# Where the split weights of a two-model fp32 kernel lie in SBUF, modulo 512 bytes

## The reference, cut to what matters

```
def swiglu(x, w_in, w_out):
    a, b = jnp.split(x @ w_in, 2, axis=-1)
    return (jax.nn.silu(a) * b) @ w_out
...
h = h + 0.5 * swiglu(rmsnorm(h, norm_ffn1), w_ffn1_in, w_ffn1_out)
fq, fk, fv, ff, rq, rk, rv, rg, ga, gb = jnp.split(u @ w_in, IN_SPLITS, axis=-1)
...
x = layer_norm(ALPHA * x + g2 * swiglu_2(modulate(x, sh2, sc2), w_ffn_in[l], w_ffn_out[l])) * ln2_g[l] + ln2_b[l]
```

## The kernel before, in words

| tile | start modulo 512 before | after |
|---|---|---|
| token tiles (X1 to X5, H1 to H4, O, MX, TH, TL) | 320 | 320 |
| Wbase, high and low | 128 | 128 |
| Wtop, high and low | 128 | 64 |
| Wlatent, high and low | 128 | 192 |
| Wmixed, high and low, and PAm | 128 | 192 |
| Wvalues, high and low | 64 | 64 |
| CS, RT | 128, 256 | 64, 192 |

## Time and profile before

### The profile page before, as it was taken

One profiled execution on the slowest core, in us unless ns is written; L12 is line 12 of the kernel. 1 busy time (PEld: TensorE's weight loads), 2 busy tenths in 40 slices (PEclk: granted clock), 3 DMA queues, 4 the chain that ended last, 5 costly groups with the idle time before them and its releaser, 6 DMA issues. The chain is left out here.

```text
span 3286.8 us, 60350 instructions
## 1 busy us (share of the span) xinstructions
PE 3163.5 (96%) x24442; PEld 2940.6 (89%) x24458; DVE 1802.9 (55%) x3099; ACT 1391.2 (42%) x2533; POOL 481.6 (15%) x471
## 2 busy tenths in 40 slices
PE   7999999999999999999999999999999999989998
PEld 7999988797778899998889888999998889979997
DVE  4666643536744456666435774222326645776765
ACT  4222232336633342224447755212125547664544
POOL 1010110036500010110103301101010103111110
PEclk9999999999999999999999999999999999999999
DMA  4445422122223244543210341221214321425653
GB/s 155 173 163 178 154 71 78 58 75 61 58 68 96 85 141 173 180 172 129 72 42 21 110 130 53 70 65 59 71 59 122 101 62 40 147 77 149 166 147 102
DMA packets 107074, 339.68 MB, mean 103 GB/s; under 512 B 12144, under 2 KB 16496, under 8 KB 106672
## 3 DMA queue, kind: packets, MB, share of 16 engines
q1 hardware_dynamic: 97616, 311.65, 29.3%
q0 software_dynamic: 8752, 23.65, 3.2%
q10 hardware_dynamic: 432, 0.52, 0.0%
HBM read 324.38 MB, written 2.10 MB: 99 GB/s over the span
## 5 line engine op out<-in xcount | busy, mean ns | idle before, releaser
L2716 DVE TENSOR_TENSOR r_Wbasel<-r_Wf,r_Wbaseh 128x1024 fp32r<-128x1024 f32 (+3 forms) x286 | 359.7, 1259 | 506.5 <-ACT r_Wbaseh L2012 506.2
L2012 ACT ACTIVATE r_Wbaseh<-r_Wf 128x1024 fp32r<-128x1024 f32 (+3 forms) x286 | 291.3, 1022 | 425.8 <-PE PS L1331 318.1
L1329 PE MATMUL PS<-r_X1h,r_Wbaseh 128*128 128x264 f32 (+1 forms) x848 | 286.6, 338 | 12.5 <-DVE r_X1l L3064 5.1
L2716 DVE TENSOR_TENSOR r_Wtopl<-r_Wf,r_Wtoph 128x1024 fp32r<-128x1024 f32 (+3 forms) x147 | 174.5, 1189 | 203.7 <-ACT r_Wtoph L2012 203.5
L1329 PE MATMUL PS<-r_X2h,r_Wbaseh 128*128 128x256 f32 (+1 forms) x888 | 274.3, 309 | 6.2 <-POOL r_X2l L3675 2.6
L1330 PE MATMUL PS<-r_X1l,r_Wbaseh 128*128 128x264 f32 (+1 forms) x848 | 273.6, 323 | 0.0
L1331 PE MATMUL PS<-r_X1h,r_Wbasel 128*128 128x264 f32 (+1 forms) x848 | 273.5, 323 | 0.0
L1330 PE MATMUL PS<-r_X2l,r_Wbaseh 128*128 128x256 f32 (+1 forms) x888 | 266.7, 300 | 0.0
L1331 PE MATMUL PS<-r_X2h,r_Wbasel 128*128 128x256 f32 (+1 forms) x888 | 266.6, 300 | 0.0
L2012 ACT ACTIVATE r_Wtoph<-r_Wf 128x1024 fp32r<-128x1024 f32 (+3 forms) x147 | 146.0, 1001 | 140.1 <-PE PS L1331 57.3
L1329 PEld LDWEIGHTS PS<-r_X1h,r_Wbaseh 128*128 128x128 f32 x848 | 160.5, 189 | 33.7 <-issue 8.0
(11 more groups left out here) (535 smaller groups left out, 10665.1 us busy)
## 6 DMA issues: line engine op xcount, KB each, us to landing
r_Wf<-in_wmod SPq DMA_DIRECT2D x96, 512.0 KB, 3.6
r_Wf<-in_f_in SPq DMA_DIRECT2D x88, 512.0 KB, 4.4
r_Wf<-in_g_in SPq DMA_DIRECT2D x69, 512.0 KB, 3.6
r_Wf<-in_w_o SPq DMA_DIRECT2D x40, 512.0 KB, 4.5
r_Wf<-in_f_out SPq DMA_DIRECT2D x32, 448.0 KB, 4.2
r_Wf<-in_g_out SPq DMA_DIRECT2D x32, 448.0 KB, 3.4
r_SR<-in_g_in SPq DMA_DIRECT2D x38, 256.0 KB, 3.5
r_SR<-in_g_in POOLq DMA_DIRECT2D x38, 256.0 KB, 5.4
```

The costliest lines, as they stand in the source:

```text
L1329: self.e.matmul(o, wh, xh, start=first, stop=False)
L2012: e.activation(p.w(i, cols)[0], p.Wf[:, i % NW, 0:cols], ACT.Copy).then_inc(*p.hi.did(i))
L2716: e.tensor_tensor(l, p.Wf[:, i % NW, 0:cols], h.bitcast(F32), ALU.subtract).then_inc(*p.lo.did(i))
```

## The change

The start of the top slots goes down by 64 bytes, and with it that of CS and RT. The start of the mixed and the latent slots goes up by 64 bytes, and with it PAm, a small tile of partial sums behind the mixed slots. No instruction is added, removed or moved, no wait changes, and the order of the work stays. The whole diff:

```diff
-TOP = 187904
+TOP = 187840
...
-        p = self.weight_slots("mixed", 3, P2 + 320)
+        p = self.weight_slots("mixed", 3, P2 + 384)
...
-        self.weight_slots("latent", 2, p + 320)
+        self.weight_slots("latent", 2, p + 384)
```

## The result

The changed kernel takes 3335.81 us (median of 4 runs, 3329.72 to 3340.27) against 3290.96 us for the kernel before in the same comparison: ratio 1.0116, 95% interval 1.0084 to 1.0148. It is slower, by 1.2% by that ratio and by 1.4% by the medians, and lies 37 us above the forecast of 3299 us and above the forecast range, which ended at 3325 us.

A forecast was written before the change was run, and what follows sets the result against it. Matmuls, busy 96% of the span, were taken to bound the kernel; +7 us for top, latent and mixed slots, 0 for the rest, on 3288.65 us gave 3295.7 us, or 3299 us as a median 3.8 us higher; range 3280 to 3325 us.

The forecast's parts named there:

- Two paces, and a stall that chooses between them: 256-column matmuls: start every 113.4 or 117.6 ns; a stall draws the pace anew, which then stays for many items.
- the term of +7 us: Top, latent and mixed slots, 6162 matmuls of 256 columns: slow share goes from 24% to 50%, +7 us.
- the bound of +20 us: Top, latent and mixed slots: if the new offset held all 4680 fast matmuls at the slow pace, +20 us.
- a pace of over 118 ns at the new offset: Undisturbed stretch: a pace under 113 or over 118 ns at the new offset would show the forecast wrong.
- The row I leaned on: First block's first stages, 264 columns: 122 ns with a moving offset against 116.7 ns estimated, 5 ns lost.
- Base slots, taken as 0: Unmoved base slots, about 6160 matmuls: 0 taken, ends of +18 us if disturbed and -9 us if freed.
- rival 3: 256-column matmuls turn slow at offset 256: +20 us for top slots alone, +38 us with base items dragged along; chance 0.22.
- Latent and mixed slots: Weight slots the change moves to 192 modulo 512: 128 from the tokens, not 256 as its description says.
- 264 columns, VectorE, ScalarE, CS, RT, PAm: nothing: Other parts: 264 columns within -3 to +3 us, VectorE's 6 ns a tile hidden, small tiles nothing.
- Waits that absorb: Stalls on late weights or splits could take back what TensorE gains or loses, 4 ns in a matmul.
- The rule of the two ports: TensorE's SBUF reads: separate ports for moving operand and weights, so the offset can't matter and the sum would be 0.
- The prediction's -26 us: Top, latent and mixed slots: if offset 256 reached the skill page's 262 cycles, 6162 x 4.2 ns = -26 us.

The follow-up runs named there:

- E5: Bare matmul stream, not the kernel: finer offsets, twelve stalls, weights moved between items, 264 and 512 columns; at 192, 113.3 or 117.8 ns a matmul.
- E1: Bare stream of three-matmul steps, not the kernel: tokens 0 to 480 bytes above weights, behind three stalls; 113.3 ns at 192, 120.0 ns at 256.
- E3: Against the kernel before: token tiles up 64 bytes, all weight slots at 128 modulo 512, so every set lies 256 from the tokens; 3343.39 us, ratio 1.0165.
- E8: Against the kernel before: only the top slots moved, 64 bytes up, to offset 128 from the tokens; 3313.37 us, ratio 1.0056.

## Why the prediction was wrong

1. **Two paces, and a stall that chooses between them.** Right. E5 has both at 192, by the stall alone.
2. **Top slots, the term of +7 us.** This is the step that failed. It said that a new offset keeps the two paces of 192 and changes at most the share of each. But 256 has a pace of its own, 120.0 ns, and no other, in every run. The true term is 33 us. Even the bound of +20 us was too low, because I took 117.6 ns for the slowest pace there is. The prediction named a pace of over 118 ns at the new offset as a sign that it was wrong, but gave it no term in the sum; the sign came.
3. **The row I leaned on.** I called the 264-column matmuls the nearest row, estimated 116.7 ns for them at rest and put the other 5 ns down to their walking offset. E5 measured 120.0 ns for 264 columns at 192 at rest. So the row said nothing about offsets. A column count is no stand-in for another one. The trace of before had no steady stream of 256 columns at 256, and I should have made the upper bound wider for that.
4. **Base slots, taken as 0.** Wrong, measured +18 us. The upper end I gave was +18 us, and the mechanism was the one rival 3 named: the items between are dragged along. It had a chance of 0.22 and is what happened, with its first part 13 us too small. That the two 18 agree is partly luck: by the mean distances about 22% of the base matmuls were slow before, not 33%, and about 82% after, not all. And the range was cut at 3325 us though rival 3 reached 3330 us; even that end lies 6 us under the result.
5. **Latent and mixed slots.** They do lie 128 from the tokens, as worked out, and not 256. Both run at 118.6 ns; together 1.5 us.
6. **264 columns, VectorE, ScalarE, CS, RT, PAm: nothing.** Right: 0.6 us on 264 columns, VectorE busy within 0.5 us.
7. **Waits that absorb.** Named as what could spoil the sum; they took 6 to 8 us of 53.
8. **The rule of the two ports.** The Trainium skill, "TensorE: Matmul & The Clock Gate", section "Step-by-step: what each phase is for", has weight loads take nothing from the running matmul. E1 measured 113.3 and 120.0 ns for the same instructions, with no other engine at work between the stalls, by the offset alone; here the measurement decides, though no run shows which read waits for which. The Trainium skill, same page, section "Back-to-back issue gap", gives the 262 cycles for a single isolated matmul and says that in a stream of weight loads and matmuls both set the spacing. The prediction's -26 us used that figure for a stream. In the streams here no offset reached 262: the least for 256 columns was 272.

Why 192 modulo 256 is the good place, what the 16, 26.7 or 32 cycles beyond the 256 are spent on, and why the return from 256 is slow when the weights move and fast when the tokens do, stays open. So does what the exchange of the two operands changes (last section). The runs show that it is so and no more.

## What to carry to other kernels

When stationary and moving operands of a long stream of fp32r matmuls have a fixed address offset, that offset modulo 256 is worth trying as a tuning parameter. Here 192 against 256 made 6% of a matmul's pace, and 1.6% of the whole kernel when every set lay at 256 (E3). Measure a bare stream at each offset, behind several stalls, for each column count in use, before laying out tiles. Keep all slots that alternate inside a stage on one offset modulo 256, since here one set at 256 slowed another that had not moved. And where the trace has no row of the new state, don't take the worst state it does have for a bound.

## What the runs showed of the hardware that I had not expected

- The pace repeats every 256 bytes: sixteen offsets from 0 to 480, the two halves equal within 0.1 ns.
- The good place is a point: 113.3 ns at 192, 120.0 at 188 and 120.0 or 122.2 at 196, each behind two stalls.
- The best place depends on the columns: for 512 it is 0 (226.7 ns against 233.5 at 192), for 256 it is 192 and 0 is among the worst, for 264 there is hardly a difference (119.9 to 122.2 ns).
- The pace of a matmul can depend on the item before it: at 192, 117.8 ns behind an item at 256 (12 of 12, and 64 of 64 in the changed kernel), 113.3 ns behind one at 128 (3 of 3 in the stream, 50 of 63 in the kernel of E8). With the tokens moved in place of the weights, E1 came back from 256 at 113.3 ns (2 of 2).
- The offset alone does not say it all. Where the roles are exchanged in the kernel before (tokens of X2 stationary, weights moving, which lie 64 above them modulo 256), the same instructions ran at 118 ns in one stretch and at 113.3 ns in another, while E1 has only 117.8 ns at 64. TensorE by stretch (length, busy and count, granted clock, DMA share, GB/s):

```profile
2679.00:2689.00 10.00, 10.00 (x87) 1.00 0.00 0
2691.00:2701.00 10.00, 10.00 (x91) 1.00 0.00 0
```

No run varied the offset of exchanged operands by itself.
